# Six of eleven Down units as seven block products, with two weight sums made by adding DMAs

## The reference

```python
h = rms_norm(x, ffn_norm[i])
u = causal_depthwise_conv(h @ w_up[i], conv_w[i], conv_b[i])
x = x + (jax.nn.silu(u[..., :D_FF]) * u[..., D_FF:]) @ w_down[i]
x = x + (p[i] @ ple_proj[i]) * jax.nn.sigmoid(x @ ple_gate[i])
```

## Time and profile before

| | us |
|---|---|
| three runs | 653.97, 655.00, 655.09 |
| median | 655.0 |
| the profiled execution | 654.48 |
| its span | 652.6 |
| PE busy | 646.1 |
| DVE busy | 534.6 |
| ACT busy | 437.8 |
| POOL busy | 192.5 |

### The profile page before, as it was taken

How to read it: one execution, slowest core, us unless ns; L and a number is a source line. 1 busy time by engine, 2 the same in 40 slices (tenths; PEclk the granted TensorE clock), 3 DMA queues, 4 the chain that set the end, 5 groups by cost and what they waited for, 6 DMA issues and landing times.

```text
span 652.6 us, 9708 instructions
## 1 busy us (share of the span) xinstructions
PE 646.1 (99%) x3762; PEld 557.9 (85%) x3762; DVE 534.6 (82%) x745; ACT 437.8 (67%) x667; POOL 192.5 (29%) x233
## 2 busy tenths in 40 slices
PE   8999999999999999999999999999999999999997
PEld 7988887888888888888889879878888888888885
DVE  5798788779989999896488777886899999998933
ACT  6769886677767776564574879856777677755532
POOL 8545510210023332206831353003000333221091
PEclk9999999999999999999999999999999999999999
DMA  9972234676655559973386421265565555699511
GB/s 322 364 264 65 69 112 152 204 239 194 193 185 190 185 201 278 312 246 109 109 301 238 160 98 65 66 199 188 194 193 189 185 187 189 204 317 306 179 32 65
DMA packets 78926, 123.25 MB, mean 189 GB/s; under 512 B 2848, under 2 KB 58912, under 8 KB 78624
## 3 DMA queue, kind: packets, MB, share of 16 engines
q1 hardware_dynamic: 74848, 114.57, 52.3%
q0 software_dynamic: 2880, 5.24, 4.4%
q10 hardware_dynamic: 1152, 2.81, 1.2%
HBM read 121.57 MB, written 1.05 MB: 188 GB/s over the span
## 4 chain that ended last, share of the span: by engine, by line
PE 96%; DVE 2%; ACT 1%; issue 0%; POOL 0%; ACTq 0%; POOLq 0%
PE ps L1716 24%; PE ps L1154 15%; PE ps L1156 14%; PE ps L1155 14%; PE ps L1718 12%; PE ps L1206 2%; PE ps L1300 1%; PE ps L1326 1%; PE ps L1566 1%; PE ps L1168 1%; PE ps L1241 1%; PE ps L1338 1%; DVE hn L2390 1%; PE ps L1777 1%; PE ps L1779 1%; PE ps L1786 1%
## 5 line engine op out<-in xcount | busy, mean ns | idle before, releaser
L1716 PE MATMUL ps<-hT_hl,wh 128*128 128x512 f32 x688 | 238.6, 392 | 0.0
L749 ACT ACTIVATE wh<-raw 128x2048 fp32r<-128x2048 f32 (+1 forms) x100 | 180.6, 1809 | 35.6 <-PE ps L1156 28.2
L1718 PE MATMUL ps<-hT_hl,wl 128*128 128x256 f32 x688 | 193.3, 281 | 0.0
L1716 PEld LDWEIGHTS ps<-hT_hl,wh 128*128 128x128 f32 x688 | 129.1, 188 | 28.2
L1718 PEld LDWEIGHTS ps<-hT_hl,wl 128*128 128x128 f32 x688 | 129.4, 188 | 0.0
L2313 DVE TENSOR_TENSOR wl<-raw,wh 128x2048 fp32r<-128x2048 f32 x44 | 102.4, 2328 | 13.6 <-ACT wh L749 13.1
L1154 PE MATMUL ps<-wh,hT_hl 128*128 128x512 f32 (+1 forms) x214 | 78.7, 368 | 0.0
L543 POOL TENSOR_TENSOR wl<-raw,wh 128x2048 fp32r<-128x2048 f32 (+1 forms) x14 | 55.5, 3974 | 73.6 <-DVE x L2379 48.8
L1156 PE MATMUL ps<-wh,hT_hl 128*128 128x512 f32 (+1 forms) x214 | 76.7, 358 | 0.0
L1155 PE MATMUL ps<-wl,hT_hl 128*128 128x512 f32 (+1 forms) x214 | 76.6, 358 | 0.0
L699 POOL TENSOR_TENSOR g_plain<-g_plain 128x128 f32<-128x128 f32 x10 | 4.7, 466 | 168.6 <-DVE g_plain L2290 168.6
(11 more groups left out here) (391 smaller groups left out, 1386.6 us busy)
## 6 DMA issues: line engine op xcount, KB each, us to landing
raw<-w_up SPq DMA_DIRECT2D x44, 1024.0 KB, 5.1
raw<-w_down SPq DMA_DIRECT2D x22, 1024.0 KB, 6.8
raw<-w_in SPq DMA_DIRECT2D x16, 1024.0 KB, 9.3
raw<-w_o SPq DMA_DIRECT2D x6, 1024.0 KB, 4.9
raw<-ple_gate SPq DMA_DIRECT2D x6, 1024.0 KB, 4.9
raw<-w_in SPq DMA_DIRECT2D x4, 704.0 KB, 5.2
raw<-w_down POOLq DMA_DIRECT2D x10, 256.0 KB, 7.1
ng<-norm_gains ACTq DMA_DIRECT2D x2, 1024.0 KB, 6.1
```

Of the source, the lines that this page charges most:

```text
L749: act.activation(w_high(u)[:, c:n], raw[:, slot, c:n], ACT.Copy).then_inc(h_made, 1)
L1716: pe.matmul(both, high[:, c], hU_all[:, k].rearrange("p a n -> p (a n)"), start=k == 0, stop=False, skip_group_check=True)
L1718: mm = pe.matmul(o, wl[:, slot, c], hU_h[:, k, :], start=False, stop=k == KT - 1, skip_group_check=True)
```

## The change

`SEVEN` takes in unit 3. For its first two units (3 and 4) POOL adds t3 to a loaded B11 by an adding DMA from SBUF to SBUF (`add_to_t2`), so that DVE makes only t4. The buffers move, so that all sums of units 3 and 4 lie outside `quarters`: in `hT`, and in a place shared with the tables `gc` and `gs`. The rounded sums get a ring of three. The sixth rounded activation (`a_high5`) takes the place of `uq` and the first 128 columns of `ukv`, and so their loads for the second layer move behind the gate loads. The diff, cut to its core (semaphore counts and allocations are left out):

```diff
-SEVEN = (4, 5, 6, 7, 8)
+SEVEN = (3, 4, 5, 6, 7, 8)
...
         def t3_sum(i):
             if i == 0:
                 return first_t3[:]
-            return quarters[:, 1536 + i * 512:1536 + (i + 1) * 512]
+            if i == 1:
+                return hT[:, 3 * KT // 4:, :].rearrange("p k n -> p (k n)")
+            return quarters[:, 1024 + i * 512:1024 + (i + 1) * 512]
...
         def t2_t4(i):
+            if i == 0:
+                return hT[:, 0:KT // 2, :].rearrange("p k n -> p (k n)")
+            if i == 1:
+                return second_t2[:]
             if 2 <= i < 4:
...
-            i %= 4
+            i -= 4
...
         def quarter_highs(i):
-            return (proj_h, pt_r)[i % 2][:, 0:1536]
+            return (pt_r, pb_r, proj_h)[i % 3][:, 0:1536]
...
                 for s in range(STEPS):
                     if s in SEVEN:
                         i = SEVEN.index(s)
-                        if i == 1:
+                        if i == 2:
                             unit_done(sp, layer, U_DOWN - 1)
                         sp.dma_start(t3_sum(i), w_down[layer][weight_rows(i, 0), 0:512]
                                      ).then_inc(F[f"b12_landed_{i}"], 16)
+                        if i < 2:
+                            sp.dma_start(t2_t4(i)[:, 0:512], w_down[layer][weight_rows(i, 0), 512:1024]
+                                         ).then_inc(F[f"b11_landed_{i}"], 16)
                     load(rows(w_down, 2 * s, 2), U_DOWN + s)
                 for n, (k, m) in enumerate(GATE_ROWS):
                     load(rows(ple_gate, k, m), U_GATE + n)
+                if layer + 1 < DEPTH:
+                    load_small_up(sp, layer + 1)
...
-                for i in range(FEW):
+                def add_to_t2(i):
+
+                    pool.wait_ge(F[f"b11_landed_{i}"], 16 * (layer + 1))
+                    pool.wait_ge(F[f"t3_made_{i}"], 16 * (layer + 1))
+                    pool.dma_start(t2_t4(i)[:, 0:512], t3_sum(i), accum_op=ALU.add
+                                   ).then_inc(F[f"t2_made_{i}"], 16)
+
+                add_to_t3(0)
+                add_to_t1(0)
+                add_to_t3(1)
+                add_to_t2(0)
+                add_to_t1(1)
+                add_to_t2(1)
+                for i in range(2, FEW):
                     add_to_t3(i)
                     add_to_t1(i)
...
                 def seven_high(i):
 
-                    if i > 1:
-                        unit_done(act, layer, U_DOWN + SEVEN[i - 2])
-                    if i == 1:
-                        act.wait_ge(F["prod"], base["prod"] + STEPS - 1)
-                        act.wait_ge(F["g_low"], base["g_low"] + eights(STEPS - 1))
-                    act.wait_ge(F["w_sums"], base["w_sums"] + 2 * i + 2)
+                    if i > 2:
+                        unit_done(act, layer, U_DOWN + SEVEN[i - 3])
+                    elif i == 2:
+                        unit_done(act, layer, U_DOWN + SEVEN[0])
+                    else:
+                        act.wait_ge(F["prod"], base["prod"] + STEPS - 1 + i)
+                        act.wait_ge(F["g_low"], base["g_low"] + eights(STEPS - 1 + i))
+                    act.wait_ge(F["w_sums"], base["w_sums"] + (2 * i if i else 1))
...
-                    unit_done(dve, layer, U_DOWN - 1 if i < 2 else
-                              U_DOWN + EARLY - 1 if i < 4 else U_DOWN + SEVEN[i - 4])
-                    dve.wait_ge(F[f"t3_made_{i}"], 16 * (layer + 1))
-                    tt(t2, t3_sum(i), raw[:, slot, 512:1024], ALU.add).then_inc(F["w_sums"], 1)
-                    dve.wait_ge(F["w_sums"], base["w_sums"] + 2 * i + 1)
+                    if i > 1:
+                        unit_done(dve, layer, U_DOWN + EARLY - 1)
+                        dve.wait_ge(F[f"t3_made_{i}"], 16 * (layer + 1))
+                        tt(t2, t3_sum(i), raw[:, slot, 512:1024], ALU.add
+                           ).then_inc(F["w_sums"], 1)
+                        dve.wait_ge(F["w_sums"], base["w_sums"] + 2 * i - 1)
+                    else:
+                        dve.wait_ge(F[f"t2_made_{i}"], 16 * (layer + 1))
                     tt(t4, t2, raw[:, slot, 1536:2048], ALU.add).then_inc(F["w_sums"], 1)
```

More of the change, by code:

```diff
@@ L152 @@
     "silu": STEPS, "prod": STEPS, "g_high": STEPS - FEW, "g_low": STEPS - FEW,
-    "w_sums": 2 * FEW, **{f"b12_landed_{i}": 16 for i in range(FEW)},
-    **{f"t{n}_made_{i}": 16 for n in (1, 3) for i in range(FEW)}, "a_sums": FEW, "a_rounded": FEW, "a_rest": FEW, "w_rounded": FEW, "w_rest": FEW,
+    "w_sums": 2 * FEW - 2, **{f"b12_landed_{i}": 16 for i in range(FEW)},
+    **{f"t{n}_made_{i}": 16 for n in (1, 3) for i in range(FEW)}, **{f"{name}_{i}": 16 for name in ("b11_landed", "t2_made") for i in range(2)}, "a_sums": FEW, "a_rounded": FEW, "a_rest": FEW, "w_rounded": FEW, "w_rest": FEW,
     "down_low": STEPS - DVE_FROM, "vector_low": 2 * STEPS - 3 + DVE_FROM, "sevens_done": 1, "sevens_copied": 2, "sevens_added": 1,
@@ L254, in build @@
         ng = sb("ng", [P, 2 * D])
+        with nc.sbuf_tensor("a_high5", [P, 7 * P], F32R) as a_high5:
+            pass
         with nc.sbuf_tensor("uq_l", [P, 2, H * QK], F32R) as uq_l:
@@ L279, in build @@
         pt = sb("pt", [P, 1536])
+        with nc.sbuf_tensor("second_t2", [P, 1024], F32) as second_t2:
+            pass
+        with nc.sbuf_tensor("second_low", [P, 1024], F32R) as second_low:
+            pass
         gc = sb("gc", [P, 4, TT, HD])
@@ L330, in g_flat @@
             return g_plain[:, n if first else n + STEPS - EARLY]
-        a_high = (a_high0, a_high1, a_high2, a_high3, a_high4)
+        a_high = (a_high0, a_high1, a_high2, a_high3, a_high4, a_high5)
         def t3_sum(i):
@@ L343, in t3_low @@
                 return ukv_h[:]
-            return hT_hl[:, 1536 + i * 512:1536 + (i + 1) * 512]
+            if i == 1:
+                return proj_h[:, 1536:2048]
+            return hT_hl[:, 1024 + i * 512:1024 + (i + 1) * 512]
         def t2_t4(i):
+            if i == 0:
+                return hT[:, 0:KT // 2, :].rearrange("p k n -> p (k n)")
+            if i == 1:
+                return second_t2[:]
             if 2 <= i < 4:
@@ L358, in quarter_sums @@
         def quarter_sums(i):
+            if i == 0:
+                return proj_h[:, 0:1024]
+            if i == 1:
+                return second_low[:]
             if 2 <= i < 4:
                 return (gT_h, gT_l)[i - 2].rearrange("p a k n -> p (a k n)")
-            i %= 4
+            i -= 4
             return hT_hl[:, i * 1024:(i + 1) * 1024]
         def quarter_highs(i):
-            return (proj_h, pt_r)[i % 2][:, 0:1536]
+            return (pt_r, pb_r, proj_h)[i % 3][:, 0:1536]
         both_sums, minus_both = (qk_swa[:, 2 * a:2 * a + 2, :].rearrange("p k n -> p (k n)")
@@ L405, in load_small, with load_small_up @@
                           ).then_inc(F["sg_landed"], 16)
+        def load_small_up(eng, layer):
             eng.dma_start(uq[:, 0, :], w_uq[layer][0:P, :]).then_inc(F["uq_landed"], 16)
@@ L472, in _ @@
                         load_small(sp, 0)
+                        load_small_up(sp, 0)
                 for n, (k, m) in enumerate(WO_ROWS):
@@ L2365, in _ @@
                     if s in SEVEN:
-                        dve.wait_ge(F["w_sums"], base["w_sums"] + 2 * SEVEN.index(s) + 2)
+                        dve.wait_ge(F["w_sums"], base["w_sums"] + max(2 * SEVEN.index(s), 1))
                     down_low(s)
```

## The result

Over 22 runs of each kernel the changed one takes 655.38 us (653.98 to 657.78), the one before 654.42 us (653.97 to 655.29). The ratio is 1.0018, with a 95% interval of 1.0011 to 1.0024: slower by about 1.2 us (the two medians lie 0.96 us apart), where 1.36 us less was forecast. It lies inside the stated range (652.8 to 656.4) and within the 0.2% that I called no change, but on the wrong side, and the interval is clear of 1. One thing stands out beside the medians: the executions of the kernel before lie within 1.3 us, those of the changed one within 3.8 us. The range alone is a weak sign: beside the later experiments single executions of the kernel before reached 656.70. The middle half of the 22 lies within 0.8 us before and 1.1 us after.

What follows compares the result with a forecast made beforehand. PE sets the time, with VectorE and the DMA engines right behind it. Six fewer matmuls give -1.36 us and all other terms 0, which puts the 655.0 us median at 653.6; range 652.8 to 656.4.

Steps and rivals of the forecast that it cites:

- The price of an add in the software queue: POOL's DMA queue: 1.44 us of all engines per 256 KB add, by packet time.
- The sum of VectorE's lead: Down stage, first layer: VectorE's operations from unit 3 on, summed without waits, put unit 8's low weights at 286.5.
- Its slack: Down stage, unit 8: low weights at 286.5, PE wants them at 287.1; 0.6 us left, stall 0.
- The moved latent loads: SP's queue at the layer boundary: four w_uq and w_ukv loads fit in a 5.6 us gap; cost 0.
- my four signs of being wrong: PE waiting for VectorE (unit 8 or 9); ACT over 2 us for raw; SBUF adds slower than HBM; shares above 1 before 247.
- the backlog: DMA engines up to 252.4: 4.3 to 6.6 us of added pieces against 4.2 free; 0 to 2.4 left, 1.0 taken.
- the limits at 2.8 and 2.2 us: Unit 8, first and second layer: lateness of t1's add beyond which PE stalls, VectorE's 0.6 us included.
- The three windows: Last two up units and unit 0, up to 252.4: DMA shares 0.69, 0.75, 0.80, leaving 4.2 us free.
- the five pieces: Added DMAs between 236 and 252: adds to t3 and t1, a B11 load, two SBUF adds; 4.3 to 6.6 us.
- (c): Unit 8: adds from SBUF dear, 3 us of all engines each, stalls of 2.8 and 3.4 us; 659.8 us; chance 0.14.
- (b): Unit 8: small stall by VectorE or t1, 0.1 to 0.7 us per layer; 653.8 to 655.0 us; chance 0.26.
- (a): The forecast itself: all cover holds, 653.6 us, give or take 0.3; chance 0.48.

## Why the prediction was wrong

**What held.** 3,756 matmuls; 0.227 us for each removed one, shown by the floor of 0.9980 (adds left out) and by 0.9979 with the adds kept and moved. The price of an add in the software queue, 1.44 us. The sum of VectorE's lead: 286.5 for the end of unit 8's low weights, 286.2 where no DMA came late. Its slack is 1.0 us instead of 0.6, and it is as scarce as I took it to be: 0.87 us less left nothing to spare, and with 2.0 us less PE started unit 8 of the first layer 1.10 us late. The moved latent loads at nothing. The chain of the stall: t1 late, ACT waiting for it, VectorE for ACT, PE for VectorE. Three of my four signs of being wrong came true: PE waiting for VectorE at unit 8, ACT waiting more than 2 us for the DMA into raw, shares above 1 before 247. The fourth did not: the adds from SBUF took 7.6 to 8.3 us to land, those from HBM 7.0 to 9.0.

**The step that failed** is the backlog: "What remains is a backlog of 0 to 2.4 us; I take 1.0." It is a term that was mis-sized, and beyond its own upper bound. t1 of unit 8 came 3.05 us late in the fastest execution; the load of unit 8 took 3.1 us longer than before in that one and 4.2 in the other profile, the load of unit 7 there 4.7. I had put the limits at 2.8 and 2.2 us, and the first was nearly right: at 3.05 us PE started unit 8 0.40 us late, which puts it at 2.65. The second limit was not put to the test: there t1 of unit 8 came 1.94 us late (603.72 against 601.78 in the earlier trace rows).

Two faults in that step show in the runs. The larger one is the price. The three windows took in nearly what I had counted on: their shares rose by 0.14, 0.31 and 0.27, 3.9 us of all engines, where I had 4.2. But four of the five pieces are adds, at 1.44 us by my own row. With them the five come to 6.6 us, and 6.6 less 3.9 leaves 2.7, near the 3.05 and 3.1 measured in the first profile; I took 1.0. My own upper bound of 2.4 already lay above the 2.2 us of room in the second layer, and I did not follow it up. The smaller fault is the place. The adds from SBUF could only go out at 244.5 and 251.6, when the shares were already at 1.06, while the window of 236 stayed at 0.83. With the early pieces moved to before 235, into free time, the load of unit 8 landed after 8.8 us again.

I also asked only who waits at unit 8. ACT waited for t1 at units 5 to 8 in both profiles, and VectorE's waits ahead of unit 8 (0.34 us at unit 6 in the first; 0.99 at unit 5 and 2.05 at unit 7 in the second) spend the same lead.

**What I left out** is the scatter. The landing of DMAs under full engines differs between executions by more than a microsecond: unit 8's load took 11.7 and 12.8 us in the two profiles, and ACT got t1 of unit 7 at 276.80 and 279.48. Any of the t1 adds of units 5 to 8 can hold PE up. By the starts the two executions lost 0.79 and 3.5 us. That the median lies between them for the same reason is likely, but no profile near it shows it. I had read the earlier trace rows, ACT waiting 0.61 us in the second layer, as room that was left; it was the sign that the landings already touched the chain.

**The rivals.** The truth was (c)'s mechanism in part and (b)'s place: DMAs late by 3 to 5 us at units 7 and 8. But (c)'s condition, adds from SBUF dear by themselves at 3 us, is not what the runs show: the same adds cost nothing early. They cost the engines 1.5 us each, like any other add, and were dear by where they stood. I had argued "the two adds fall early, where the shares are below 1", which the page after contradicts: 1.06 and 1.07. (a) had 0.48; it does hold for the version with the early DMAs.

## What to carry to other kernels

A transfer that takes work off a busy engine takes the same time of the DMA engines wherever it stands; what it costs the kernel depends on who waits behind it. Put such transfers into a stretch where the DMA share is well under 1, even if their results are needed much later. Price each piece by its own queue's packet time: here an add cost nearly twice a load of the same bytes. Where a landing already ends just when it is asked for, count it as a limit. And look at the spread of the executions, since one profile can be of the fastest, and at PE's starts, since idle time before a row can understate a stall.

## What the runs showed of the hardware

- An instruction of POOL on two SBUF inputs of 128x512 (1.62 us) stretched VectorE's two-input operation beside it from 2.28 to 3.21 us, another from 0.68 to 1.78. An add by DMA in its place stretched none of them: the longest of the 44 of 128x2048 in the up stages took 2.59 us in the changed kernel and 2.59 in the kernel before.
- With 1024 bytes for descriptors POOL's fourth open add of 256 KB waited until the first had landed (4.56 us at the longest in one profile, 5.14 in the other); with 2048 bytes it did not.
- Adds of 256 KB cost 1.44 us of all 16 engines in either kernel, by the packets' time, and plain loads of the same size 0.78. Those from SBUF cost 1.5. They took 5.1 to 9.4 us from issue to landing in the three profiles of the two kernels.
